# One sum and one root for two neighbouring RMS norms in a two-layer hybrid block (GLA, stick-breaking attention, RWKV-7), with the update of x put off

## The reference, cut to what matters

```python
def rmsnorm(x, g):                      # the same in both models, EPS = NORM_EPS = 1e-6
    y = xf * lax.rsqrt(jnp.mean(xf * xf, axis=-1, keepdims=True) + EPS)
    return y * g

# end of the odd layer, then the closing norm of the first model
x = x + gate_res * (y @ out_w)
x = rmsnorm(x, final_g)
# the second model: the residual stream is that x, and all projections read h
h = rmsnorm_2(x, mix_pre_norm)
z = h @ w_in                            # attention, RWKV and gate columns
...
x = x + rmsnorm_2(mixed @ w_out, mix_post_norm)
```

## Time and profile before

| | us |
|---|---|
| runs | 1004.1, 1004.41, 1005.12 |
| median | 1004.41 |
| the profiled execution, its time | 1003.99 |
| its span | 1002.2 |
| granted TensorE clock, mean | 0.997 of full |
| TensorE matmul busy | 974.6 (97% of the span) |
| VectorE busy | 642.0 (64%) |
| ScalarE busy | 518.6 (52%) |
| weights and inputs read | 170.03 MB |

### The profile page before, as it was taken

One profiled execution on the slowest core, in us unless ns is written; L12 is line 12 of the kernel. 1 busy time (PEld: TensorE's weight loads), 2 busy tenths in 40 slices (PEclk: granted clock), 3 DMA queues, 4 the chain that ended last, 5 costly groups with the idle time before them and its releaser, 6 DMA issues.

```text
span 1002.2 us, 19946 instructions
## 1 busy us (share of the span) xinstructions
PE 974.6 (97%) x8871; PEld 943.0 (94%) x8871; DVE 642.0 (64%) x731; ACT 518.6 (52%) x606; POOL 1.1 (0%) x11
## 2 busy tenths in 40 slices
PE   7999999999999999999999999999979999999998
PEld 6899999989999998999999999899869999999998
DVE  3887887764775555654689855256665666466565
ACT  3345454346444579744583541267636654354445
POOL 0000000000000000000000000000000000000000
PEclk9999999999999999999999999999999999999998
DMA  9999557945576443567235442124215366556521
GB/s 341 366 366 305 163 168 254 304 120 167 191 241 200 127 139 115 169 194 233 73 99 167 129 127 85 44 86 168 95 64 173 122 201 220 170 182 198 182 89 43
DMA packets 153441, 172.36 MB, mean 172 GB/s; under 512 B 4000, under 2 KB 137692, under 8 KB 153228
## 3 DMA queue, kind: packets, MB, share of 16 engines
q1 hardware_dynamic: 151696, 167.43, 51.5%
q10 hardware_dynamic: 1660, 3.67, 1.0%
HBM read 170.03 MB, written 1.05 MB: 171 GB/s over the span
## 4 chain that ended last, share of the span: by engine, by line
PE 49%; DVE 7%; ACT 3%; issue 2%; DVEq 0%
PE pj L2450 37%; DVE w_lo L1353 1%; ACT w_hi L890 1%; PE m_all L2175 1%; PE m_all L2177 1%; PE m_all L2164 1%; PE pj L2409 1%; PE pj L2411 1%; PE pj L2410 1%; PE m_all L1906 1%; PE pj L2266 1%; PE m_all L1900 1%; PE m_all L2300 1%; DVE work L1727 0%; PE m_all L1927 0%
## 5 line engine op out<-in xcount | busy, mean ns | idle before, releaser
L1353 DVE TENSOR_TENSOR w_lo<-raw,w_hi 128x2048 fp32r<-128x2048 f32 (+2 forms) x128 | 288.0, 2253 | 158.9 <-ACT w_hi L890 158.1
L2450 PE MATMUL pj<-h_hi,w_hi 128*128 128x256 f32 x1232 | 350.0, 284 | 5.9 <-DVE h_lo L1736 3.0
L2450 PE MATMUL pj<-h_hi,w_lo 128*128 128x256 f32 x1232 | 344.1, 279 | 0.0
L2450 PE MATMUL pj<-h_lo,w_hi 128*128 128x256 f32 x1232 | 343.9, 279 | 0.0
L890 ACT ACTIVATE w_hi<-raw 128x2048 fp32r<-128x2048 f32 (+2 forms) x128 | 240.0, 1877 | 116.9 <-PE pj L2450 82.8
L2450 PEld LDWEIGHTS pj<-h_hi,w_hi 128*128 128x128 f32 x1232 | 230.2, 187 | 12.4 <-issue 8.7
L2450 PEld LDWEIGHTS pj<-h_lo,w_hi 128*128 128x128 f32 x1232 | 230.3, 187 | 0.4
L2450 PEld LDWEIGHTS pj<-h_hi,w_lo 128*128 128x128 f32 x1232 | 230.1, 187 | 0.2
L2450 PE MATMUL pj<-y_hi,w_hi 128*128 128x256 f32 x600 | 168.6, 281 | 3.2 <-DVE y_lo L1820 3.1
L2450 PE MATMUL pj<-y_hi,w_lo 128*128 128x256 f32 x600 | 167.6, 279 | 0.0
L2450 PE MATMUL pj<-y_lo,w_hi 128*128 128x256 f32 x600 | 167.4, 279 | 0.0
(11 more groups left out here) (365 smaller groups left out, 1201.1 us busy)
## 6 DMA issues: line engine op xcount, KB each, us to landing
raw<-in_odd_in_w_dram SPq DMA_DIRECT2D x28, 1024.0 KB, 5.3
raw<-in_w_in_dram SPq DMA_DIRECT2D x23, 1024.0 KB, 5.3
raw<-in_ada_w_dram SPq DMA_DIRECT2D x22, 1024.0 KB, 7.9
raw<-in_w_ff_in_dram SPq DMA_DIRECT2D x16, 1024.0 KB, 5.4
raw<-in_w_ff_out_dram SPq DMA_DIRECT2D x16, 1024.0 KB, 5.1
raw<-in_even_in_w_dram SPq DMA_DIRECT2D x13, 1024.0 KB, 5.3
raw<-in_even_out_w_dram SPq DMA_DIRECT2D x8, 1024.0 KB, 6.1
raw<-in_odd_out_w_dram SPq DMA_DIRECT2D x8, 1024.0 KB, 5.1
```

The source lines that it names most:

```text
L1353: V.tensor_tensor(w_lo[:, i % SPL, 0:n], raw_of(u)[:, 0:n], w_hi[:, i % SPL, 0:n].bitcast(F32), ALU.subtract).then_inc(S(f"split{i % SPL}" ...
L2450: m = nc.tensor.matmul(to, a_, b_, start=(s == 0 and q == 0 and (fb == 0 or not together)), stop=(s == len(steps_) - 1 and q == 2), skip_g ...
```

## The change

It replaces the two norms by one sum and one root, and orders the rest anew:
- `final_norm` behind the four `oo` jobs becomes `final_part` q behind each job q. On ScalarE it squares the two chunks of x that the job ended; the DMAs and the table load now stand in part 0, ahead of its square. VectorE forms in part 0 the gains final_g · mix_pre_norm and the matrix rows `gain_rows` (ones times final_g² + EPS), and in each part it multiplies the two chunks of x by the joint gain into `work`. TensorE adds the squares of job q-1 to a weighted sum in M[0] behind job q.
- `mix_pre`: TensorE adds the first two chunks of the plain sum (M[1]), the last two of the weighted sum, then the other six of the plain sum. ScalarE takes the joint root of the weighted sum, copies the `h_hi`, and only then takes the plain root. VectorE multiplies the eight chunks by the joint root (a tensor_tensor) and subtracts behind two of them rather than three.
- `final_norm` keeps only VectorE's eight instructions on x and stands ahead of the job `wga` 1.
- Both `keep_busy` steps are gone.

```diff
-BUSY = {"norm1": (8, 2), "final": (9, 2), "mix": (10, 2), "ffn": (8, 2), "gate": (7, 2)}
+BUSY = {"norm1": (8, 2), "ffn": (8, 2), "gate": (7, 2)}
...
-    proj("oo", "residual", ins["odd_out_w"][0], 0, 4, 8, lambda xc: ("y_lo", 8 + (xc - 8) // 2 + 1), kparts=2)
-    step("final_norm")
-    step("keep_busy", "final")
+    for i in range(4):
+        us = [unit(ins["odd_out_w"][0], KD * kp, KD, i * CB, CB) for kp in range(2)]
+        job("oo", "residual", i, "F", us, KD, 8, lambda xc: ("y_lo", 8 + (xc - 8) // 2 + 1))
+        step("final_part", i)
...
     step("mix_pre")
-    step("keep_busy", "mix")
...
     step("solve_y", 1)
+    step("final_norm")
     second("wga", "sigmoid", 4000, 1)
...
+            pool.memset(eps_square_col, EPS * EPS).then_inc(S("scalars_set"), 1)
...
             # ScalarE
+            def final_part(q):
+                if q == 0:
+                    act.wait_ge(S("sb_arg"), SB_H)
...
+                    act.preload_act_table_set(LOG_EXP)
+                evacuated(act, ("oo", q))
+                nc.scalar.activation(ar(S_["sq"] + 2 * q, 2), x[:, 2 * q:2 * q + 2, :], ACT.Square).then_inc(S("squares"), 1)
...
             def mix_pre():
-                squares(3, x, S_["sq"], lambda e, q: e.wait_ge(S("x_update"), 2 * q + 2))
+                act.wait_ge(S("sum_sq"), 3)
+                link(nc.scalar.activation(both_roots, M[0][:, 0:T], ACT.Ln, bias=eps_square_col, scale=1.0 / D))
+                nc.scalar.activation(both_roots, both_roots, ACT.Exp, scale=-0.5).then_inc(S("rstd"), 1)
                 upper(2)
+                act.wait_ge(S("sum_sq"), 4)
+                link(nc.scalar.activation(rstd[:, :], M[1][:, 0:T], ACT.Ln, bias=eps_col, scale=1.0 / D))
+                nc.scalar.activation(rstd[:, :], rstd[:, :], ACT.Exp, scale=-0.5).then_inc(S("rstd"), 1)
...
             # VectorE
+            def final_part(q):
+                if q == 0:
+                    dve.wait_ge(S("sb_y"), SB_H)
+                    V.tensor_tensor(both_gains, vec("final_g", 0, 8), vec("mix_pre_norm_2", 0, 8), ALU.mult)
+                    link(V.tensor_tensor(gain_square, vec("final_g", 0, 8), vec("final_g", 0, 8), ALU.mult))
+                    link(V.tensor_scalar(gain_square, gain_square, EPS, None, ALU.add))
+                    for k in range(KD):
+                        i_ = V.tensor_scalar(gain_rows[k], K("ones"), gain_square[:, k:k + 1], None, ALU.mult)
...
+                evacuated(dve, ("oo", q))
+                for k in (2 * q, 2 * q + 1):
+                    i_ = V.tensor_scalar(normed_at(2)[:, k, :], x[:, k, :], both_gains[:, k:k + 1], None, ALU.mult)
...
             def final_norm():
-                projected(dve, ("oo", 3))
-                dve.wait_ge(S("rstd"), 3)
+                dve.wait_ge(S("rstd"), 4)
...
             def mix_pre():
-                apply_norm(3, 2, x[:, :, :], normed_at(2), lambda k: vec("mix_pre_norm_2", k))
+                dve.wait_ge(S("rstd"), 3)
+                dve.wait_ge(S("scaled"), scaled[0])
+                for k in range(KD + 2):
+                    if k < KD:
+                        V.tensor_tensor(normed_at(2)[:, k, :], normed_at(2)[:, k, :], both_roots, ALU.mult).then_inc(S("normed"), 1)
+                    if k >= 2:
+                        lower(2, k - 2)
...
             # TensorE
-            def final_norm():
-                sum_squares(2, O_["sq"])
+            def weighted(q):
...
+                for k in (2 * q, 2 * q + 1):
+                    m = nc.tensor.matmul(M[0][:, 0:T], gain_rows[k], ar(S_["sq"] + k)[:, 0, :], start=(k == 0), stop=(k == KD - 1), skip_group_check=True)
+                return m
+            def plain(q):
...
+                    m = nc.tensor.matmul(M[1][:, 0:T], K("ones"), ar(S_["sq"] + k)[:, 0, :], start=(k == 0), stop=(k == KD - 1), skip_group_check=True)
...
+            def final_part(q):
+                if q >= 1:
+                    weighted(q - 1)
...
             def mix_pre():
-                sum_squares(3, S_["sq"])
+                plain(0)
+                weighted(3).then_inc(S("sum_sq"), 1)
+                for q in range(1, 4):
+                    m = plain(q)
+                m.then_inc(S("sum_sq"), 1)
```

More of the change, by code:

```diff
@@ L129 @@
 WORK, SPARE = 58, 100
-S_ = dict(sq=0, h=8, r=40, k=36, v=SPARE + 12, xx=56, lora=52,
+S_ = dict(gw=16, sq=0, h=8, r=40, k=36, v=SPARE + 12, xx=56, lora=52,
           sw=12, a=8, cs=SPARE + 28, cc=SPARE + 24, er=SPARE, kk=SPARE + 4, rn=SPARE + 8, kt=SPARE + 16, rk=SPARE + 16,
@@ L678, in program @@
         gn_eps_col = small[:, 42:43]
+        eps_square_col = small[:, 43:44]
+        both_gains, gain_square = small[:, 20:28], small[:, 28:36]
         token_rstd = small[:, 60:62]
@@ L693, in program @@
         ffn_eps = s0_flat
+        both_roots = s0_flat
+        gain_rows = [flat(S_["gw"], 4)[:, k * P:(k + 1) * P] for k in range(KD)]
         log_decay = -KAPPA
@@ L950, in norm @@
                 upper(n)
-            def final_norm():
[L954 to L962, removed]
+            def final_part(q):
+                if q == 0:
+                    act.wait_ge(S("sb_arg"), SB_H)
+                    act.wait_ge(S("sb_y"), SB_H)
+                    act.wait_ge(S("gla_states"), GLA_H)
+                    act.dma_start(cst_phase[:, 0:CONST_PLACES[3][1]], consts[:, CONST_AT[3]:CONST_AT[4]]).then_inc(S("late_in"), 16)
+                    act.dma_start(lora[0:32, 0, :], ins["rwkv_w2_2"][0]).then_inc(S("late_in"), 16)
+                    act.dma_start(lora[32:64, 0, :], ins["rwkv_a2_2"][0]).then_inc(S("late_in"), 16)
+                    act.dma_start(lora[0:96, 1, :], ins["rwkv_g2_2"][0]).then_inc(S("late_in"), 16)
+                    act.preload_act_table_set(LOG_EXP)
+                evacuated(act, ("oo", q))
+                nc.scalar.activation(ar(S_["sq"] + 2 * q, 2), x[:, 2 * q:2 * q + 2, :], ACT.Square).then_inc(S("squares"), 1)
             def sgu_v():
@@ L1291, in evac @@
                     nc.scalar.activation(y_hi[:, c:c + 2, :], gate_tmp("yt", g), ACT.Copy).then_inc(S("y_hi"), 1)
-            act.wait_ge(S("scalars_set"), 3)
+            act.wait_ge(S("scalars_set"), 4)
             run(steps, evac, split_to, "hi")
@@ L1437, in norm @@
                 apply_norm(n, n, x[:, :, :], normed_at(n), lambda k: mod[:, n, k:k + 1], lambda k: ada_c[:, n, k:k + 1])
+            def final_part(q):
[6 more added lines that the diff above has]
+                        i_ = V.tensor_scalar(gain_rows[k], K("ones"), gain_square[:, k:k + 1], None, ALU.mult)
+                    i_.then_inc(S("scaled"), 1)
+                    scaled[0] += 1
+                evacuated(dve, ("oo", q))
+                for k in (2 * q, 2 * q + 1):
+                    i_ = V.tensor_scalar(normed_at(2)[:, k, :], x[:, k, :], both_gains[:, k:k + 1], None, ALU.mult)
+                i_.then_inc(S("scaled"), 1)
+                scaled[0] += 1
             def final_norm():
-                projected(dve, ("oo", 3))
-                dve.wait_ge(S("rstd"), 3)
+                dve.wait_ge(S("rstd"), 4)
                 for k in range(KD):
@@ L1560, in fold @@
                 for q in upto:
-                    dve.wait_ge(S("squares"), 4 * STATS[name][0] + q + 1)
+                    dve.wait_ge(S("squares"), 4 * (STATS[name][0] - 1) + q + 1)
                     if q == 3:
@@ L1891, in evac @@
                     done_reading(ins_, key)
-            dve.wait_ge(S("scalars_set"), 3)
+            dve.wait_ge(S("scalars_set"), 4)
             run(steps, evac, split_to, "lo", lambda u: ada_to(u + 1))
@@ L1945, in norm @@
                     sum_squares(1, O_["sq"])
-            def final_norm():
-                sum_squares(2, O_["sq"])
+            def weighted(q):
+                pe.wait_ge(S("squares"), 8 + q + 1)
+                if q == 0:
+                    pe.wait_ge(S("scaled"), 9)
+                for k in (2 * q, 2 * q + 1):
+                    m = nc.tensor.matmul(M[0][:, 0:T], gain_rows[k], ar(S_["sq"] + k)[:, 0, :], start=(k == 0), stop=(k == KD - 1), skip_group_check=True)
+                return m
+            def plain(q):
+                for k in (2 * q, 2 * q + 1):
+                    m = nc.tensor.matmul(M[1][:, 0:T], K("ones"), ar(S_["sq"] + k)[:, 0, :], start=(k == 0), stop=(k == KD - 1), skip_group_check=True)
+                return m
+            def final_part(q):
+                if q >= 1:
+                    weighted(q - 1)
             def sgu_w():
@@ L2043, in mean_square @@
                 if last:
-                    pe.wait_ge(S("squares"), 4 * STATS[name][0] + 4)
+                    pe.wait_ge(S("squares"), 4 * (STATS[name][0] - 1) + 4)
                     for c in range(6, 8):
@@ L2071, in ple_post @@
                                          start=(c == 0 and tt == 0), stop=False, skip_group_check=True)
-                pe.wait_ge(S("squares"), 4 * STATS["e"][0] + 4)
+                pe.wait_ge(S("squares"), 4 * (STATS["e"][0] - 1) + 4)
```

(2 more changed lines are left out.)

4 lines of the change are left out of this document (2 added, 2 removed).

## The result

| | before | changed |
|---|---|---|
| median of the runs, us | 1004.25 (1003.9 to 1005.12, 4 runs) | 997.34 (996.92 to 997.99, 4 runs) |
| ratio | | 0.9933, 95% interval 0.9917 to 0.9949 |
| profiled execution, us | 1003.99 | 997.37 |
| its span | 1002.2 | 995.5 |

A forecast was written before the change was run, and what follows sets the result against it. TensorE, busy in 97% of the span, was taken as the bound; at the join 18.12 - 9.6 - 1.73 = 6.8 us saved, giving 997.6 us from the median of 1004.41, range 996.5 to 1000.4.

The forecast's parts named there:

- The place to read: Join from job `oo` 3 to chunk 7 of `wx`, 18.12 us before; what it saves should reach the end.
- The sum and the root: At the join: weighted sum complete at 2.94 us, VectorE's first product after the root at 3.99 us.
- 0.34 per product: VectorE's chain at the join: each tensor_tensor product takes 0.34 us; upper bound the old 0.40, 0.5 us more in all.
- The stream: Weighted pairs 0 and 1 behind jobs 1 and 2 add 1.73 us to TensorE, all on the path.
- the allowance for changes between kinds of matmul: Behind jobs 1 and 2 on TensorE: 0 to 0.3 us extra at each of the two places.
- Hidden work: Added ScalarE and VectorE work behind jobs 0 to 2, plain root and deferred update: all claimed to cost nothing.
- The splits behind the jobs: Behind jobs 0 to 2, later splits stay covered by 3 us in part 0, about 5 in the others: no cost.
- the plain root: ScalarE's Ln and Exp behind its last copy, 0.9 us, hidden; its next split is over 8 us ahead.
- the deferred update: Eight updates of x, 3.25 us, hidden in VectorE's 9.29 us idle before `wga` 1; rival, not hidden: 1000.9 us, chance 0.03.
- the clock's case: Rival at the join: TensorE's clock falls in the new gaps, costing 2.6 us, time 1000.2 us; chance 0.07.
- the rival that I named: Clock falls to 0.50 in the join's new gaps, time 1000.2 us; chance 0.07.
- The rival's price: Cost of the clock falling at the join: 5.2 us of low clock, half of it lost, 2.6 us.

## Why the prediction was right

- *The place to read.* The chain of waits and the timeline of one join, taken against each other to a fixed matmul, gave a sum that came out whole in the time: 6.75 us in the traces, 6.7 between the spans, 6.9 between the medians. The reason is what the view of waits had shown: TensorE has next to no wait behind the join. That it came out to a tenth is in part luck, since in both profiled executions the clock stayed up there behind the join; in the four where it fell at 498 to 503, the stretch to the end was 0.8 to 1.3 us longer than in the changed kernel.
- *The sum and the root.* 3.99 us to VectorE's first product were predicted; measured 474.62 - 470.57 = 4.05.
- *VectorE.* 0.34 per product, 5.10 us from the first product to the last `h_lo`: measured 4.36 to the start of the last `h_lo` but two (478.98 - 474.62), from where the last one starts two instructions later (the three take 1.09, the last of them 0.42): 5.03. The reason that I had for the 0.34, the form of the instruction, was not the reason: the other form runs as fast without its column operand.
- *The stream.* 1.73 us predicted, 1.72 measured; the allowance for changes between kinds of matmul (up to 0.3 us each) was not needed.
- *Hidden work.* The splits behind the jobs, the plain root and the deferred update cost nothing, each in the idle time that was named for it. 6.20 us of idle time are left in the solve, about 6 were forecast.
- *The clock.* Here the prediction was right by less than it claimed. It held the clock's case unlikely because a stretch of 54% busy time at 744.80 to 751.50 stayed at 1.00, and called it nearly the same. It is not. There TensorE waited about 1 us once in twelve matmuls; at the join it waits some 0.3 us behind every three, and the view that gave 54% (3.62 of 6.70 us) gives 91% at the join (4.35 of 4.80), because a row of 0.28 us covers much of such a gap:

```profile
475.80:480.60 4.80, 4.35 (x27) 2.67 (x27) 4.27 (x13) 3.50 (x10) 0.00 (x0) 1.00 0.00 0
```

The changed kernel stayed at 1.00 over the whole join. But in the trace with the plain sum's twelve rows gone, the same stretch ended at 0.50. So the rival that I named was avoided, as far as one trace can tell, because the plain sum fills the wait ahead of `wx`, a role that the prediction did not see in it. The rival's price was wrong too. I took 5.2 us of half clock and half of it as cost, 2.6; it was 3.4 us, of which half is 1.7, and it cost 1.09, because as long as TensorE waits for VectorE half of the time, half the clock costs little: it costs only from where the waits end.
- *The clock rule cited.* By "TensorE: Matmul & The Clock Gate" in the Trainium skill, section "A second HAM failure mode: psum-queue depth-cycling", short idles between groups can bring the clock down. In the changed kernel the trace does not show it: 1.00, with short waits behind every three matmuls. In the one with the rows left out the clock did fall, to 0.50 from about 479 on, but a wait of 2.57 us stood ahead of the short ones, so that trace does not tell which of the two brought it.

## What to carry to other kernels

Where two reductions follow each other on one chain, look for the algebra that makes one root of both, and then ask separately which of the remaining work still has a consumer on the chain: here the second root and sum gave one half of the gain and the update that could wait the other half. Spreading a reduction over the busy stream ahead of the join is not free when the engine of the reduction is the one that bounds the stream; put it where that engine waits, or give it to an engine that has idle time. And matmuls that look hidden may be what keeps the clock up: before they are taken out of a wait, read the granted clock behind it, not only their cost, and in more than one execution.

## What was not expected of the hardware

- In the one trace without them, the join was longer once hidden matmuls were taken out. Each in one trace, waits of 3.22 and 3.28 us with nothing on TensorE were followed by 0.50 of the clock (1.2 GHz); one of 2.57 us followed by half-busy work was too, though only in that work; one of 1.71 us followed by full work was not, nor was one of 2.67 us between the two sums of the kernel before without its idle matmuls. At half the clock a matmul of 256 columns took 0.21 us from start to start where it takes 0.12.
- With the same matmuls ahead of it, 0.03 us apart, the clock fell to 0.50 for 3.4 us at 498 in one execution and stayed at 1.00 in another.
- A scalar_tensor_tensor of 128x256 f32 with an immediate scalar took 416 ns, one with a column of SBUF as scalar 476 ns (on other tiles), and a tensor_tensor 420 ns.
- Matmuls of 64 and 96 columns can be taken in turn into one PSUM bank, the wider first with the start flag, at the usual 0.117 us from start to start.
